# A fused two-block kernel on one core: eight low weight parts on GpSimd, a changed order on VectorE, a root on ScalarE, scores of four heads at once

## The reference

```python
def reference(...):
    x = first_block(...)     # depth 1
    return second_block(x, ...)

def first_block(...):
    mem_n = rmsnorm(mem, norm_mem_w)
    h = x + head_group_mixer(rmsnorm(x), ...)         # conv of width 31 and retention, 8 heads
    h = h + memory_cross_attention(rmsnorm(h), mem_n) # 4 heads, 256 memory tokens
    h = h + sq_relu_mlp(rmsnorm(h))                   # 1024 -> 4096 -> 1024
    return rmsnorm(h, norm_f_w)

def retention(q, k, v, positions):      # heads of 32 (q, k) and 64 (v)
    scores = einsum('bnihd,bnjhd->bnhij', rotary(q), rotary(k)) * decay_in
    ...                                 # times v, plus the state carried between chunks of 64

def second_block(...):
    x = x + hybrid_mixer(rms_norm(x))   # stick-breaking attention (a running sum), a spatial
                                        # gating unit, a gated conv of width 3; three gated branches
    x = x + memory_cross_attention_2(rms_norm(x), mem)
    x = x + swiglu(rms_norm(x))         # hidden width 2816
    return rms_norm(x, final_g)
```

## Time and profile before

| what | us |
|---|---|
| median of three runs (926.34 to 926.68) | 926.49 |
| time of the profiled execution | 928.6 |
| its span | 926.5 |
| PE busy in the span | 911.3 (98%) |
| PE weight loads, busy beside the matmuls | 800.3 (86%) |
| DVE busy | 658.0 (71%) |
| ACT busy | 497.6 (54%) |
| POOL busy | 25.3 (3%) |
| DVE on low parts of whole slabs (L1631, 147 of them, 2.29 each) | 335.5 |
| ACT on high parts (L1164, 147 of them, 1.91 each) | 280.4 |

### The profile page before, as it was taken

How to read it: one execution, slowest core, us unless ns; L and a number is a source line. 1 busy time by engine, 2 the same in 40 slices (tenths; PEclk the granted TensorE clock), 3 DMA queues, 4 the chain that set the end, 5 groups by cost and what they waited for, 6 DMA issues and landing times.

```text
span 926.5 us, 13108 instructions
## 1 busy us (share of the span) xinstructions
PE 911.3 (98%) x5304; PEld 800.3 (86%) x5304; DVE 658.0 (71%) x918; ACT 497.6 (54%) x571; POOL 25.3 (3%) x69
## 2 busy tenths in 40 slices
PE   8999999999999999999999999999999999999996
PEld 8988999889888888888998978888899888888885
DVE  6699999788676666656866877655686676565666
ACT  6686435474555444444646638744465554544443
POOL 1510010000000000000000000000000000000000
PEclk9999999999999999999999999999999999999999
DMA  8656455445356566654655435555453455666551
GB/s 326 228 179 226 148 194 182 162 157 168 105 167 197 181 187 197 204 183 155 231 182 182 141 135 180 175 174 195 137 185 132 138 182 185 191 197 199 181 181 46
DMA packets 101281, 164.40 MB, mean 177 GB/s; under 512 B 2736, under 2 KB 70960, under 8 KB 100976
## 3 DMA queue, kind: packets, MB, share of 16 engines
q1 hardware_dynamic: 100384, 161.09, 53.0%
q0 software_dynamic: 560, 1.84, 0.6%
q10 hardware_dynamic: 288, 0.79, 0.2%
HBM read 162.65 MB, written 1.05 MB: 177 GB/s over the span
## 4 chain that ended last, share of the span: by engine, by line
PE 90%; DVE 6%; DMA 1%; ACT 1%; issue 1%; SPq 0%; DVEq 0%
PE ps L585 21%; PE ps L587 21%; PE ps L586 21%; PE ps L629 14%; PE ps L633 7%; DVE w_lo L1631 2%; PE ps L720 1%; DVE c_acc L1776 1%; DMA w_ring<-in_xkv_w 1%; DMA w_ring<-in_head 1%; ACT w_hi L1164 0%; PE ps L757 0%; DVE acc L2135 0%; ACT c_out L1348 0%; PE ps L849 0%
## 5 line engine op out<-in xcount | busy, mean ns | idle before, releaser
L1631 DVE TENSOR_TENSOR w_lo<-w_ring,w_hi 128x2048 fp32r<-128x2048 f32 x147 | 335.5, 2288 | 119.4 <-ACT w_hi L1164 118.3
L1164 ACT ACTIVATE w_hi<-w_ring 128x2048 fp32r<-128x2048 f32 x147 | 280.4, 1910 | 96.8 <-DMA w_ring<-in_w_in 32.4
L629 PE MATMUL ps<-xx,w_hi 128*128 128x512 f32 x576 | 137.2, 390 | 0.2
L629 PEld LDWEIGHTS ps<-xx,w_hi 128*128 128x128 f32 x576 | 106.8, 188 | 22.0 <-issue 0.7
L585 PE MATMUL ps<-w_hi,xx 128*128 128x512 f32 x304 | 121.2, 399 | 2.6 <-DVE w_lo L1631 2.2
L586 PE MATMUL ps<-w_lo,xx 128*128 128x512 f32 x304 | 119.2, 392 | 0.0
L587 PE MATMUL ps<-w_hi,xx 128*128 128x512 f32 x304 | 119.0, 392 | 0.0
L585 PE MATMUL ps<-xx,w_hi 128*128 128x256 f32 x384 | 110.2, 287 | 1.3 <-DVE w_lo L1631 0.8
L586 PE MATMUL ps<-xx,w_hi 128*128 128x256 f32 x384 | 109.3, 285 | 0.0
L587 PE MATMUL ps<-xx,w_lo 128*128 128x256 f32 x384 | 109.3, 285 | 0.0
L585 PE MATMUL ps<-w_hi,ff_h 128*128 128x512 f32 (+1 forms) x218 | 84.7, 389 | 0.0
(11 more groups left out here) (324 smaller groups left out, 1305.7 us busy)
## 6 DMA issues: line engine op xcount, KB each, us to landing
w_ring<-in_w_in SPq DMA_DIRECT2D x34, 1024.0 KB, 5.1
w_ring<-in_mlp_up_w SPq DMA_DIRECT2D x16, 1024.0 KB, 5.5
w_ring<-in_mlp_down_w SPq DMA_DIRECT2D x16, 1024.0 KB, 4.9
w_ring<-in_w_gate_ffn SPq DMA_DIRECT2D x11, 1024.0 KB, 5.3
w_ring<-in_w_up_ffn SPq DMA_DIRECT2D x11, 1024.0 KB, 5.4
w_ring<-in_w_down_ffn SPq DMA_DIRECT2D x11, 1024.0 KB, 4.9
w_ring<-in_xkv_w SPq DMA_DIRECT2D x8, 1024.0 KB, 5.3
w_ring<-in_w_out SPq DMA_DIRECT2D x8, 1024.0 KB, 4.9
```

The costliest lines, as they stand in the source:

```text
L629: pe.matmul(feat(bank + b), wh[:, k, b * P:(b + 1) * P], xx[:, k, :, :].rearrange("p e t -> p (e t)"), start=k == 0, stop=False)
L1164: act.activation(w_hi[:, s, :], w_ring[:, s, :], ACT.Copy).then_inc(hi_done, 1)
L1631: dve.tensor_tensor(w_lo[:, s, :], w_ring[:, s, :], w_hi[:, s, :].bitcast(F32), ALU.subtract).then_inc(lo_done, 1)
```

## The change

POOL_LOW names eight slabs whose low part POOL now writes, in two groups of four: the first four behind its last constant, the others behind its small loads. PE waits for those by a semaphore of their own. On DVE those eight are left out. The rest of the diff: the low values come before four taps; `ret_scores` makes four heads at a time, once for key slab 0 and once for key slab 2; one low part stands ahead of the running sum, and the `early` step of slab I_C3 + 5 stands behind the short convolution; at the end ACT takes a square root, and DVE a reciprocal and one Newton step.

```diff
+POOL_LOW = (9, 11, 17, 19, 22, 23, 25, 27)
+        def low_ready_at(i, step=0):
+            if i in POOL_LOW:
+                return pool_lo, POOL_LOW.index(i) + 1
+            return lo_done, weight_count(i) - sum(j < i for j in POOL_LOW) + step
 # POOL
+            def lo(i):
+                s = PLACE[i]
+                pool.wait_ge(hi_done, weight_count(i))
+                pool.tensor_tensor(w_lo[:, s, :], w_ring[:, s, :], w_hi[:, s, :].bitcast(F32), ALU.subtract).then_inc(pool_lo, 1)
+                pool.wait_ge(pool_lo, POOL_LOW.index(i) + 1)
             pool.wait_ge(dist_set, 1)
+            for i in POOL_LOW[:4]:
+                lo(i)
             pool.wait_ge(s_dec_ready, RET_HEADS)
...
+            for i in POOL_LOW[4:]:
+                lo(i)
 # PE
-                    pe.wait_ge(lo_done, weight_count(i) + step)
+                    pe.wait_ge(*low_ready_at(i, step))
...
+            def ret_scores(f):
+                heads = range(4 * f, 4 * f + 4)
+                for hd in heads:
+                    pe.wait_ge(*((s_dec_ready, hd - 3) if f else (v1_lo, hd + 1)))
+                rows = [slice(RET_DK * (hd % 4), RET_DK * (hd % 4 + 1)) for hd in heads]
+                for b, r in enumerate(rows):
+                    pe.matmul(tok(b)[:, 0:S], qkT[r, 2 + f, 0:P], qkT[r, f, 0:S], start=True, stop=True)
+                for b, r in enumerate(rows):
+                    pe.matmul(tok(b)[:, S:S + P], qkT[r, 2 + f, P:S], qkT[r, f, P:S], start=True, stop=True).then_inc(ret_s, 1)
                 keys(I_K1 + j, j % 2, m_t)
-                ret_scores(2 * j)
-                ret_scores(2 * j + 1)
+                if j % 2 == 0:
+                    ret_scores(j // 2)
 # ACT, at the end
+            def last_root(tb):
+                act.wait_ge(sum_ready, tb + 1)
+                act.activation(ny[:, tb:tb + 1], nv[:, tb:tb + 1], ACT.Sqrt).then_inc(root_ready, 1)
+            act.activation(warm, ones[:, 0:1], ACT.Sqrt)
             last_square(0, 0)
             last_square(0, 1)
-            for part in range(3):
-                last_square(1, part)
+            last_root(0)
+            last_square(1, 0)
             last_scale(0, 0)
+            last_square(1, 1)
+            last_square(1, 2)
+            last_root(1)
             last_scale(1, LEAD)
 # DVE
-            lo(9)
...
-            lo(11)
...
             lo(16)
+            value_rests(0, v1_lo)
             conv(4)
-            value_rests(0, v1_lo)
-            lo(17)
...
-                lo(18 + j)
+                if j != 1:
+                    lo(18 + j)
...
-            lo(22)
-            lo(23)
-            lo(25)
-            lo(27)
...
+                lo(I_C3 + 2 * j + 3)
                 early(I_C3 + 2 * j)
-                lo(I_C3 + 2 * j + 3)
...
-                if k == 0:
-                    early(I_C3 + 5)
             after(dve.tensor_tensor(acc3[:, :, :], acc3[:, :, :], ...))
+            early(I_C3 + 5)
...
+            def inverse_root(tb):
+                v, y, t = (x[:, tb:tb + 1] for x in (nv, ny, nt))
+                dve.wait_ge(root_ready, tb + 1)
+                after(dve.reciprocal(y, y))
+                after(dve.tensor_scalar(t, v, y, y, ALU.mult, ALU.mult))
+                after(dve.scalar_tensor_tensor(y, t, -3.0, y, ALU.add, ALU.mult))
+                dve.sem_inc(y_ready, 1)
```

More of the change, by code:

```diff
@@ L321, in build @@
         hi_done, lo_done, slab_used = sem("hi_done"), sem("lo_done"), sem("slab_used")
+        pool_lo = sem("pool_lo")
+        def low_ready_at(i, step=0):
+            if i in POOL_LOW:
+                return pool_lo, POOL_LOW.index(i) + 1
+            return lo_done, weight_count(i) - sum(j < i for j in POOL_LOW) + step
         chunk_loaded = [sem(f"chunk_loaded{m}") for m in range(4)]
@@ L366, in build @@
         gate_ready, merge_done, merged_hi, merged_lo = sem("gate_ready"), sem("merge_done"), sem("merged_hi"), sem("merged_lo")
-        last_sq, y_ready, out_lead, out_tail, stored = (sem(x) for x in ("last_sq", "y_ready", "out_lead", "out_tail", "stored"))
+        last_sq, sum_ready, root_ready, y_ready, out_lead, out_tail, stored = (sem(x) for x in ("last_sq", "sum_ready", "root_ready", "y_ready", "out_lead", "out_tail", "stored"))
         u_scaled = sem("u_scaled")
@@ L683, in form_b_half @@
                 for j in range(2):
-                    pe.wait_ge(lo_done, weight_count(i0 + j))
+                    pe.wait_ge(*low_ready_at(i0 + j))
                     wh, wl = slab(i0 + j, HALF)
@@ L1085, in _ @@
                         merged_transpose(0, tok)
-                    pe.wait_ge(lo_done, weight_count(i + 2))
+                    pe.wait_ge(*low_ready_at(i + 2))
                     wh, wl = slab(i + 2, HALF)
@@ L2264, in partial @@
                 return [sq_last[:, 2 * tb + part:2 * tb + part + 1] for part in range(3)]
-            after(dve.tensor_scalar(gain[:, :], gain[:, :], -1.0 / 256, None, ALU.mult))
-            v, y, t = ([x[:, tb:tb + 1] for tb in range(TB)] for x in (nv, ny, nt))
+            after(dve.tensor_scalar(gain[:, :], gain[:, :], -16.0, None, ALU.mult))
             last_add(0, 0)
@@ L2271, in _ @@
             gained(0, 1)
-            last_add(1, 0)
             dve.wait_ge(last_sq, 2)
             s = partial(0)
-            after(dve.scalar_tensor_tensor(v[0], s[0], D * EPS, s[1], ALU.add, ALU.add))
-            column_rsqrt(v[0], y[0], t[0])
-            dve.sem_inc(y_ready, 1)
+            dve.scalar_tensor_tensor(nv[:, 0:1], s[0], D * EPS, s[1], ALU.add, ALU.add).then_inc(sum_ready, 1)
+            last_add(1, 0)
+            inverse_root(0)
             last_add(1, 1)
@@ L2281, in _ @@
             gained(1, 1)
-            gained(1, 2)
             dve.wait_ge(last_sq, 4)
             s = partial(1)
-            after(dve.scalar_tensor_tensor(v[1], s[0], D * EPS, s[1], ALU.add, ALU.add))
+            after(dve.scalar_tensor_tensor(nv[:, 1:2], s[0], D * EPS, s[1], ALU.add, ALU.add))
             dve.wait_ge(last_sq, 5)
-            after(dve.tensor_tensor(v[1], v[1], s[2], ALU.add))
-            column_rsqrt(v[1], y[1], t[1])
-            dve.sem_inc(y_ready, 1)
+            dve.tensor_tensor(nv[:, 1:2], nv[:, 1:2], s[2], ALU.add).then_inc(sum_ready, 1)
+            gained(1, 2)
+            inverse_root(1)
             c = slice(0, LEAD)
-            dve.scalar_tensor_tensor(xn[:, 1, c], h[:, 1, c], y[1], gain[:, c], ALU.mult, ALU.mult).then_inc(out_lead, 1)
+            dve.scalar_tensor_tensor(xn[:, 1, c], h[:, 1, c], ny[:, 1:2], gain[:, c], ALU.mult, ALU.mult).then_inc(out_lead, 1)
 def kernel(**inputs):
```

## The result

The changed kernel took 931.84 us (median of five), the kernel before 926.53 beside it; 932.5 was forecast. One of the five, the execution first profiled, was disturbed and took 4262 us: it counts in that median, but not in the ratio, and the profile after is of the same kernel in its second set of runs. The ratio is 1.0046, with a 95% interval of 1.0031 to 1.0061. The change makes the kernel slower, by 4.3 us by the ratio and 5.3 by the medians. The second set has a median of 930.45, a ratio of 1.0043 (1.0029 to 1.0057), and a profiled execution of 932.22 with a span of 930.4.

The account below looks back on a forecast made before the run. PE, busy 98% of the span, bounds the kernel, so only its standing or lower clock counts. 926.5 - 4.9 (order) - 0.7 (root) + 7.9 (POOL's delays, scores included) + 3.7 (clock) = 932.5; own range 928 to 938, with rivals 918.5 to 939.

Parts of the forecast that it names:

- The order: Running sums, 510 to 555 us: reordering removes PE waits of 0.9 and 2.4 and 1.6 of lower clock, gain 4.9.
- The root: End of the kernel: the root on ACT shortens the chain of small DVE steps, gain 0.7, bounds 0.2 and 1.1.
- The scores: Four heads at once save PE two pairs, 1.7, but for heads 4 to 7 the saving goes into a wait.
- The hold: Each POOL subtraction of 2048 elements keeps DVE's operations with both inputs in SBUF off for 4.0 us.
- (b): Slabs 17 and 19: POOL delays taps and decays; PE stands 2.9 before heads 4 to 7's scores, net loss 1.1.
- Rival 1: POOL's long operation does not keep DVE off, so no loss from POOL's parts: 918.7 us; chance 0.28.
- (a): Slab 9: POOL gets in behind a tap, and PE stands 4.0 us before its transposes near 56.
- (c): Slabs 23, 25, 27: small chain +1.4; PE stands 1.1 for low part 26 and 1.8 at column sums, together 2.8.
- The clock: PE runs at its lower clock behind the new stands: 1.6 + 1.6 + 0.5 = 3.7 us lost.
- The sum: Whole kernel: 926.5 - 4.9 - 0.7 + 7.9 + 3.7 = 932.5 us; chance 0.55.

Follow-up runs that it names:

- experiment 5: The changed kernel without POOL's eight low parts, with VectorE's old order around the running sums put back: 924.10 us, ratio 0.9967.
- experiment 3: The kernel before with only the eight low parts moved to POOL: 936.75 us, ratio 1.0107.
- experiment 2: The changed kernel with all eight low parts back on VectorE, in their old places: 918.17 us, ratio 0.9913.
- experiment 7: The changed kernel without POOL's eight low parts, with scores made two heads at a time again: 920.57 us, ratio 0.9934.
- experiment 10: The changed kernel with slab 23 alone on POOL, the other low parts on VectorE: 920.45 us, ratio 0.9933.
- experiment 9: The changed kernel with slab 9 alone on POOL, the other seven low parts on VectorE: 923.61 us, ratio 0.9962.
- experiment 12: The changed kernel with slab 22's low part back on VectorE, seven slabs on POOL: 928.83 us, ratio 1.0026.
- experiment 4: The changed kernel with only slab 9's low part back on DVE: 933.30 us, ratio 1.0077.
- experiment 8: The changed kernel with slabs 9, 11 and 23 back on VectorE, POOL keeping 17, 19, 22, 25 and 27: 926.24 us, ratio 0.9998.

## Why the prediction was right, step by step

**The order (4.9 forecast).** Measured 5.0 (uncertain by 1.8), and waits of 2.2 and 0.9 came and went as forecast. Right. The part of it that is clock is not lost in every execution; where it is not, a wait of 0.9 for sb_c that the prediction did not have comes in its place (experiment 5).

**The root (0.7, bounds 0.2 to 1.1).** Too small: 1.45 by the traces. Beside the earlier trace rows, before:
```profile
918.46 0.28 PE L587 MATMUL ps<-w_hi,ff_l 128*128 128x256 f32 x1
918.67 1.27 DVE L2255 SCALAR_TENSOR_TENSOR h<-ps,stat,h 128x512 f32<-128x512 f32 x2 [0.17 <-DVE stat L2249]
```
The prediction's 917.3 for PE's last matmul was a misreading; it began at 918.46, so the tail was 8.0 and became 6.6. Two terms: from h of the last half to the last scaling 4.07 became 3.23 us, 0.84, which is about my term. The other 0.61 I did not see: the root of the *first* half stood in front of that h. That h began 0.21 after the start of PE's last matmul before, and now begins 0.40 ahead of it (923.42 against 923.82).

**The scores (1.7, lost in a wait).** The size holds, 0.87 for four heads, where two took 0.86. The rule of the Trainium skill, "TensorEngine Tiling (Array Packing)", section "Theoretical Speedup", that the prediction cites holds as far as the trace goes: four ran in the time of two. Without POOL's parts it is won (1.9, with a wait of 0.7 before the first four). In the changed kernel it did go into a wait, but not the one forecast: PE reaches ry's transposes earlier, and stands 4.28 there where it stood 2.73 with POOL's parts alone (experiment 3). The 1.6 between them is what four heads at a time take off DVE's lead (experiments 2 and 7). It is a reading of the traces; no run has the changed kernel with pairs.

**The hold (4.0).** Its kind was right, its size low: 4.55 to 4.62 us wherever POOL did not itself wait. By the Trainium skill, "GPSIMD Engine Reference", section 3.1, 4497 ns: the trace agrees within 3%. The lock of "SBUF — State Buffer", section "Who interferes with whom", shows too, down to an operation of 128 x 16. With 4.5 for the hold my working gave 936.5, about 5 more than measured, mostly because it had 3.7 of standing in (b) that did not come. Rival 1 (DVE goes on, 918.7) is refuted by the tap of 4.83 us; its time is that of the kernel without POOL's parts.

**(a) Slab 9, 4.0.** 4.4, at the place forecast.

**(b) Slabs 17 and 19, 2.9.** This step failed. It said that POOL gets in behind a tap as soon as it has its input. At slab 19 POOL waited 2.4 us until DVE read PSUM, so the delay fell behind the decays, and PE stood 0 where 2.9 was forecast. Cut in four, POOL did get in among the taps, and PE stood 3.5 at just the place that (b) names.

**(c) 1.4 within the slack, then 1.1 and 1.8.** The wrong path: no wait came at either place, and PE stood 4.28 before ry's transposes, which the prediction passed over. For xx it counted 2.2 us of subtraction taken out; for ry that is no help, since slab 23's subtraction stood behind ry. What helps there is DVE's lead, 2.4 us with slab 23 alone (experiment 10) or with slab 9 alone (experiment 9). With all eight it is 0.1 (4.33 of hold, 4.28 of standing), so the slabs between have used it up, and the whole hold reached PE. Experiment 12 has the same without slab 22 (3.01 of hold, 2.96 of standing), which leaves slabs 11 to 19. The 1.8 exists: 1.83 in experiment 12, where PE comes earlier.

**The clock (3.7).** About right by the medians, low by the traces. Between the profiled executions of the changed kernel and the one without POOL's parts, PE lost 1.7 behind slab 9 beyond the stand (transposes of qkr at 66.72 against 60.77, less 4.28), up to 3.3 between 116 and 181, and 1.6 between 181 and 205: 6.6. But these two lie 14.8 apart and the medians 12.3, so 4 is a fairer estimate (6.6 less 2.5).

**The sum.** The forecast's +11.6 for POOL's parts already has the 1.7 of the scores taken off. Taken apart as the runs are, it says +13.3 for POOL's parts and -7.3 for the rest; measured about +12 and -8.1. The rest was low by the root's 0.75. In POOL's parts, the forecast of 9.8 us of standing (4.0, 2.9, 1.1, 1.8) met 9.2 in the trace (4.44, 0.44, 4.28), but 5.8 of the forecast did not come and 4.3 came at a place that it did not name. That these nearly cancel was luck. The number was better than its reasons: it was right that POOL's subtractions keep DVE off, nearly for how long, and that PE pays for it at slab 9.

## What to carry to other kernels

Work moved from VectorE to GpSimd is no relief when both read SBUF with two inputs: a 128x2048 subtraction of 4.6 us kept VectorE off for up to 4.4 us to save it 2.3. It held taps, subtractions and the smallest TENSOR_SCALAR; operations that read PSUM, and a TENSOR_REDUCE, ran on. Count such a move as a delay of the full GpSimd time at the worst place within its reach, in both directions; cutting it in four made this kernel 3 us slower. For every place where PE takes something from VectorE, read how far VectorE is ahead there: that lead is the reserve, and a saving on PE shortens it. Judge parts singly only with the others in place: a slab that costs nothing behind another's stand can cost once that one is mended (experiments 4, 8 and 12).

## What was not expected of the hardware

- VectorE can keep GpSimd off for long: 6 us behind ten taps and a subtraction in close order (10.47 us for an operation of 4.6). In the changed kernel GpSimd's operations of slabs 11, 19, 22 and 25 took 5.7 to 7.0 us and ended 4.5 to 4.6 after VectorE had left its row of taps. Yet at slab 9 GpSimd got in behind the first tap, and cut in pieces it took turns with the taps. What decides who gets in between closely spaced operations stays open.
- The clock fell behind stands of 4.4 and 4.3 us. It stayed full behind one of 1.85, and behind 2.2 us it fell in one execution and not in another. In experiment 8 it stayed full behind 3.40 us (1.00 in 137 to 142) and fell behind 2.35 (0.57 in 169 to 173), so the length of the stand alone does not tell. At 185 to 195 it was 0.86 and 0.79 with no long wait just before; that was not explained.
